# Six value-row buffers in place of eight, and six kept selection weight units in place of four, in a two-block transformer kernel

## The reference, cut to what matters

```python
def peer(h, w_query, sub_keys, u, v):        # per chunk of 16 tokens
    q = einsum('btd,dq->btq', hx, w_query)   # 1024 -> 2048
    s = einsum('bthpc,hpnc->bthpn', q, sub_keys)
    ...                                      # top-16 per half, then top-16 of 256
    u_sel = take(u, expert, axis=0)          # 128 rows of 1024 per token
    v_sel = take(v, expert, axis=0)
    act = gelu(einsum('btd,bthkd->bthk', hx, u_sel))
    return einsum('bthk,bthkd->btd', gate * act, v_sel)
```

## Time and profile before

| | |
|---|---|
| Median of 3 runs | 2071.33 us (2069.29 to 2072.9) |
| Profiled execution | 2071.07 us |
| Span of that execution, first to last instruction | 2069.3 us |
| TensorE / VectorE / ScalarE / GpSimd busy | 86% / 66% / 41% / 50% |
| Moved by DMA | 704.86 MB, of which the gathers 553.72 MB |
| Gathers | 528 of u and 528 of v |
| Ring loads | 246 |

### The profile page before, as it was taken

How to read it: one execution, slowest core, us unless ns; L and a number is a source line. 1 busy time by engine, 2 the same in 40 slices (tenths; PEclk the granted TensorE clock), 3 DMA queues, 4 the chain that set the end, 5 groups by cost and what they waited for, 6 DMA issues and landing times.

```text
span 2069.3 us, 21820 instructions
## 1 busy us (share of the span) xinstructions
PE 1787.2 (86%) x6516; PEld 1010.4 (49%) x6516; DVE 1356.4 (66%) x2953; ACT 846.8 (41%) x2015; POOL 1044.7 (50%) x1064
## 2 busy tenths in 40 slices
PE   9899777779988787797989878977778999989998
PEld 6565222213344452244546424422223986778996
DVE  4577988556488569847956975355554566558874
ACT  3344434330157134314732434344333445546653
POOL 0666777775567657755766676667773000000000
PEclk9999999999999999998999999999999999999999
DMA  7999999999999999999999999999996744445564
GB/s 279 366 407 408 409 409 409 406 398 368 378 403 381 409 409 409 409 410 386 384 399 409 409 409 409 409 406 409 410 409 261 232 157 122 135 147 150 189 185 132
DMA packets 194709, 704.86 MB, mean 341 GB/s; under 512 B 21769, under 2 KB 23313, under 8 KB 194337
## 3 DMA queue, kind: packets, MB, share of 16 engines
q0 software_dynamic: 152064, 553.72, 67.9%
q1 hardware_dynamic: 40816, 147.51, 20.6%
q10 hardware_dynamic: 1712, 2.24, 0.3%
HBM read 701.66 MB, written 1.06 MB: 340 GB/s over the span
## 4 chain that ended last, share of the span: by engine, by line
PE 43%; DMA 29%; POOL 10%; DVE 8%; issue 6%; ACT 2%; ACTq 0%; DVEq 0%; SPq 0%; POOLq 0%
PE ps L950 18%; DMA a<-in_peer_v,eidx 16%; DMA a<-in_peer_u,eidx 13%; PE ps L668 12%; POOL a L498 5%; PE ps L574 5%; POOL a L510 5%; DVE a L1916 3%; PE ps L691 3%; PE ps L813 2%; DVE ring_r L2100 1%; PE ps L703 1%; PE ps L627 0%; DVE a L2054 0%; PE ps L560 0%
## 5 line engine op out<-in xcount | busy, mean ns | idle before, releaser
L668 PE MATMUL ps<-a,diag 128*128 128x512 f32 (+1 forms) x1880 | 911.5, 617 | 217.0 <-DMA a<-in_peer_v,eidx 178.8
L1916 DVE SCALAR_TENSOR_TENSOR a<-a,ps 128x1024 f32<-128x1024 f32 x512 | 621.4, 1218 | 378.8 <-DMA a<-in_peer_u,eidx 359.1
L668 PEld LDWEIGHTS ps<-a,diag 128*128 128x128 f32 (+1 forms) x1880 | 331.3, 190 | 743.3 <-issue 651.6
L498 POOL DMA_INDIRECT a<-in_peer_u,eidx x528 | 525.5, 995 | 311.2 <-DVE a L1916 143.1
L510 POOL DMA_INDIRECT a<-in_peer_v,eidx x528 | 518.4, 982 | 221.4 <-issue 123.3
L1269 ACT ACTIVATE gel<-dots 128x1 f32<-128x1 f32 x528 | 104.3, 201 | 691.8 <-DVE a L1916 686.8
L950 PE MATMUL ps<-a_r 128*128 128x256 f32 (+1 forms) x1624 | 381.1, 328 | 6.2 <-DVE a_r L2324 2.4
L950 PEld LDWEIGHTS ps<-a_r 128*128 128x128 f32 x1624 | 270.2, 189 | 37.7 <-DVE a_r L2324 2.8
L2100 DVE TENSOR_TENSOR ring_r<-wring,a_r 128x1024 fp32r<-128x1024 f32 x139 | 169.6, 1222 | 127.4 <-ACT a_r L1523 127.1
L1523 ACT ACTIVATE a_r<-wring 128x1024 fp32r<-128x1024 f32 x139 | 146.3, 1053 | 71.0 <-PE ps L950 62.2
L1281 ACT ACTIVATE diag<-cstc,cga 128x128 f32<-128x128 f32 (+1 forms) x398 | 158.3, 398 | 13.3
(11 more groups left out here) (292 smaller groups left out, 1550.0 us busy)
## 6 DMA issues: line engine op xcount, KB each, us to landing
wring<-in_units SPq DMA_DIRECT2D x246, 512.0 KB, 4.4
a<-in_peer_u,eidx POOLq DMA_INDIRECT x528, 12.9
a<-in_peer_v,eidx POOLq DMA_INDIRECT x528, 13.0
late<-in_units SPq DMA_DIRECT2D x8, 512.0 KB, 15.5
a<-in_units SPq DMA_DIRECT2D x7, 512.0 KB, 14.6
a<-in_poolm SPq DMA_DIRECT2D x1, 1632.0 KB, 8.5
late<-in_cs SPq DMA_DIRECT2D x1, 1280.0 KB, 7.6
h<-in_xin SPq DMA_DIRECT2D x2, 512.0 KB, 4.3
```

Of the source, the lines that this page charges most:

```text
L498: g.indirect_dma_start(ug[:, n % NU, :], None, peer_u, bass.IndirectOffsetOnAxis(ap=eidx[:, t, k:k + 1], axis=0))\
L668: last = nc.tensor.matmul(ps[0:P, b + j, :], diag[:, pe_slots[n] % ND, 0:P], vg[:, k % NV, j * 512:(j + 1) * 512], start=False, stop=n == ...
L1916: v.scalar_tensor_tensor(ug[:, n % NU, :], ug[:, n % NU, :], 1.0, hnm if t == 2 else ps2(4), ALU.mult, ALU.mult, accum_out=dots[:, k % 8:k ...
```

## The change

Two of the eight v buffers are given up. Their 2048 words a partition, which lie behind the six others in `a1`, become `kept_too`, places for two more kept units; `a1` keeps its size. Units 10 to 15 of the query projection are now loaded once for both fronts. The two new ones (10 and 11) are loaded by SyncE in the start of the kernel, behind the last of the units with places of their own, with no wait ahead of them; units 12 to 15 go to `late` as before, at their place in SyncE's order. The v buffer of slot n is now n modulo 6, and a v gather waits for the slot six before it. The semaphore `kept` counts six loads. The ring carries four units less: two in front A, two in front B.

```diff
-NV = 8
+NV = 6
+NK = 6
...
-        A1W = (NU + NV) * 1024
+        A1W = (NU + NV + NK - 4) * 1024
...
-        vg = a1[:, NU * 1024:A1W].rearrange("p (n d) -> p n d", d=1024)
+        vg = a1[:, NU * 1024:(NU + NV) * 1024].rearrange("p (n d) -> p n d", d=1024)
...
+        kept_too = a1[:, (NU + NV) * 1024:A1W].rearrange("p (n d) -> p n d", d=1024)
...
-        KEPT = {U0["wq" + x] + 12 + m: m for x in "AB" for m in range(4)}
+        KEPT = {U0["wq" + x] + 16 - NK + m: m for x in "AB" for m in range(NK)}
...
             if n in KEPT:
-                return kept[:, KEPT[n]:KEPT[n] + m, :]
+                k = KEPT[n]
+                return kept_too[:, k:k + m, :] if k < NK - 4 else kept[:, k - NK + 4:k - NK + 4 + m, :]
...
+                if n == U0["wq"] + 14:
+                    for m in range(NK - 4):
+                        k = U0["wqA"] + 16 - NK + m
+                        sp.dma_start(kept_too[:, m, :], units[in_dram[k], :, :]).then_inc(S("kept"), 16)
...
                 if n in KEPT:
-                    if n < U0["wqB"]:
+                    if n < U0["wqB"] and KEPT[n] >= NK - 4:
                         sp.wait_ge(S("sc0_pe"), PEER_H + 1)
                         sp.dma_start(weights(n)[:, 0, :], units[in_dram[n], :, :]).then_inc(S("kept"), 16)
...
-            def sums_slot(P, k, n, vfill, b=6):
+            def sums_slot(P, n, b=6):
...
-                pe.wait_ge(S(f"v{k % NV}"), vfill)
+                pe.wait_ge(S(f"v{n % NV}"), 16 * (n // NV + 1))
...
-                                            vg[:, k % NV, j * 512:(j + 1) * 512], start=False,
+                                            vg[:, n % NV, j * 512:(j + 1) * 512], start=False,
```

More of the change, by code:

```diff
@@ L684, in beside @@
             def beside(base):
-                return Beside(lambda k: sums_slot(128, k, base + k, 16 * ((base + k) // NV + 1)), LAG)
+                return Beside(lambda k: sums_slot(128, base + k), LAG)
             def q_unit(w, j, a, b):
@@ L764, in _ @@
             for k in range(16):
-                sums_slot(META, k, m_base + k, 16 * ((m_base + k) // NV + 1), META_BANK)
+                sums_slot(META, m_base + k, META_BANK)
             sums_end(2, 2, META_BANK)
```

## The result

The changed kernel takes 2084.55 us (median of 4 runs, 2083.63 to 2089.76), the kernel before 2070.54 us in the same series: a ratio of 1.0074, interval 1.0062 to 1.0085, or 14 us slower. Forecast were 2076.3 us and a range of 2066 to 2081 us: the sign was right, the size was not. The profiled execution took 2083.63 us, with a span of 2081.8 us against 2069.3.

What follows compares the result with a forecast made beforehand. Full DMA engines were taken as the bound, in some not-full stretches TensorE or GpSimd's issues. Front A -2.6 + 1.1 = -1.5, front B +3.3 + 3.4 = +6.7, together +5.2 on 2071.1: 2076.3 us, range 2066 to 2081.

Steps and rivals of the forecast that it cites:

- The wait where TensorE is the bound, cost 0: 480 to 570 us: later v gathers cost 0, covered by full TensorE and VectorE's 12.5 us wait; uncovered +5.1 us.
- Rival 3: 480 to 570 us: VectorE's lost lead is not swallowed, coefficients reach TensorE late, 5.1 us on top: 2081 us; chance 0.12.
- Slot 306, +3.3: Front B, gather issued at 968.4 us: refill lands at 979.0 instead of 975.7, +3.3 us, bounds 0 and 4.3.
- three places are left: Only at slots 194, 306 and 363 does the refill land later than before: +1.1, +3.3 and +3.4 us.
- Slot 363, +3.4: Front B's query units: issue waits until 1142.5 us, lands at 1148.7 instead of 1145.3, +3.4 us that stays.
- Front B's -2.6: Two ring loads fewer in front B save 2.6 us of DMA time, counted as nothing because the queue runs empty.
- Front A's -2.6: Two ring loads fewer in front A's burst, where DMA is full, come out whole: -2.6 us.
- Slot 194, +1.1: Gather issued at 611.4 us moves to 614.7, lands at 620.9 instead of 619.8: +1.1 us that stays.
- The prologue's loads, cost 0: Two added loads, issued at some 24 us, find room before the first gather at 50 us: cost 0; uncovered +2.6 us.
- Full stretches, cost 0: Where DMA is full, six v buffers just cover its pace and later gathers stand shorter in the queue: cost 0.
- the 405 that the prediction named as a sign of being wrong: A rate below 405 GB/s in the full stretches would show six buffers too few for the pace.
- The fit of the Trainium skill: 2.0 us and bytes / 436e3, 3.2 us per gather; the three costs would be 0, 0.3 and 0.4 us; not used.

Runs made afterwards that it cites:

- depth alone: Six v buffers instead of the eight of the kernel before, four kept units as there, nothing loaded in the prologue: 2087.59 us, ratio 1.0074.
- experiment 4: Kernel before, with only the v gathers of slots 194, 306 and 363 to 365 also waiting for the slot six before: 2077.14 us, ratio 1.0039.
- v6_clean: Six v buffers and four kept units against the kernel before, in a series where that took 2070.92 us: 2087.59 us (2 runs), ratio 1.0074.
- front A alone: Kernel before, with only the v gathers of slots 150 to 190 also waiting for the slot six before: 2075.17 us, ratio 1.0022.
- seven and seven: Seven u and seven v buffers in place of six and eight, four kept units, against the kernel before: 2074.3 us, ratio 1.0022.
- v6: Six v buffers, four kept units, the rest as in the changed kernel; against the kernel before, ratio 1.0043 in the first series, later 1.0074.
- experiments 2 and 1: Both ran six v buffers with four kept units against the kernel before: 2 gave 1.0074; 1, where DMA was short, 1.0037 to 1.0064.
- experiments 4 and 6: 4: three places' v waits tightened in the kernel before, 1.0039. 6: V_BEHIND 3 and 1 in the changed kernel, 1.0053 and 1.0144; 3 in the kernel before, 1.0057.
- v6_again: Repeat of six v buffers and four kept units against the kernel before, in a series where that took 2179.79 us: ratio 1.0037.

## Why the prediction was wrong in size

Point by point, by its steps:

- **The wait where TensorE is the bound, cost 0: this step failed.** It measured +6.4 us (6.6 in depth alone, 4 to 5 with the stretch tightened alone, 2 to 7 by that experiment's interval). The text had the right quantity, two slots less ahead, 4 gathers, 5.1 us, and then let VectorE's 12.5 us wait swallow it. That wait gave VectorE its time back, not the DMA engines. They are full behind it, 410 GB/s in 570 to 603 us, so 5.4 us of gathers that were not moved are still missing when VectorE's 30 us of work on rows in hand are used up. Rival 3 had the place and nearly the price; its condition (VectorE's lag not swallowed, so coefficients late at TensorE) was half right: the lag was swallowed, but the rows were late, the v rows at TensorE (2.52 us) and the u rows at VectorE (4.47 us), and behind these a coefficient too (2.33 us for 1.07). TensorE waited for none of it inside the stretch.
- **Slot 306, +3.3: the place was right, the term too small.** Alone it gives 4.0 up to slot 328, by the lateness of GpSimd's stream and not of its own row. But the whole stretch gives +8 in the changed kernel, where slot 327 waits again, between the slots 320 and 332 that have no slack. The prediction took "three places are left" from times of before, in which a slot with slack counts as safe; slack is spent by the delay before it.
- **Slot 363, +3.4: right in size,** +3.5 measured, +3.6 alone, with the luck told in experiment 4.
- **Front B's -2.6 counted as lost: right.** The changed kernel's lead over v6_clean does not grow in front B, it falls from 4.1 to 2.4 us.
- **Front A's -2.6: 4.1 us at slot 290** by the same comparison, of which 2.4 us survive front B; both are differences of two executions, good to some 2 or 3 us.
- **Slot 194, +1.1: wrong, 0 in the ladder.** In experiment 4 its refill was issued at 614.1 us and landed after 5.6 us, not 6.2, at 619.7 us; before it was 619.8.
- **The prologue's loads, cost 0: right.** Issued at 24.9 us, landed at 39.7 and 41.3, in the gap where the rate rose from 64 to 140 GB/s; the first gather comes at 49.6 us, and slot 150 ends 0.2 us later than before.
- **Full stretches, cost 0: right in 76 to 460 us** (407 GB/s, v rows landing after 10.9 us in 250 to 350 us, 11 forecast), not quite in 676 to 960: 405 GB/s, with the dip at 860 to 930 us whose cause is open. Its 16 x 70 us = 1.12 MB are 2.7 us by the division above, but the ladder moves by 0.8 us only from slot 240 to 290. 1060 to 1580 us has 404, below the 405 that the prediction named as a sign of being wrong; the 79 x 35 us = 2.8 MB missing in 1130 to 1165 us, slot 363's dip, account for it.
- **The fit of the Trainium skill** ("DMA: Bandwidth & Descriptors", "Anatomy of one DMA") would have made the three places cheaper still, 0.7 us. Slot 363's refill in experiment 4 landed after 4.1 us, the quickest of all v gathers of that trace, still above its 3.2; the measured terms of 4.0 and 3.6 us decide against it.

The missing 9 us, by the changed kernel's ladder: 6.4 for the first step; less 1.1 for slot 194; nothing for front A (from +6.4 at slot 186 to +3.8 at 305, the forecast 2.6); 4.9 for front B's stretch (from 3.8 to 12.0, 8.2 for 3.3); 0.1 for slot 363; less 1.2 that come back behind slot 372, for which no run gives a reason. That is 9.1; 5.2 + 9.1 = 14.3 us, the ladder's last row. It is a sum over one execution and closes by its making; the experiments bear out its two large terms, the first step and front B's stretch.

## What to carry to other kernels

In this kernel, whose gather phase ends with full DMA queues, the price of a buffer was near the DMA time that the engines stood idle more, and neither an engine that was busy all through the stretch nor a wait that another engine had in it hid it. Read the GB/s column of a full-TensorE stretch as a debt that the next saturated stretch may not repay. As an estimate it is good to 1 to 3 us here: 5.1 us for v6_clean's first stretch (6.6 in the ladder), 6.5 for front A alone (3.8 to 4.9), 4.5 for seven and seven (3.1), and 2.7 against 0.8 in 860 to 930 us. When places of small slack are listed, walk them in order with the delay already accumulated, and look for the consumers that use a row the moment it lands.

## What was not expected of the hardware

- The DMA engines moved 405 GB/s in 76 to 460 us in one trace of the kernel of `v6` and 366 in another (experiments 2 and 1). The mean granted clock of TensorE over these executions was 0.973 and 0.946. It is not the chip: on one and the same the kernel before took 2070.1 and 2164.16 us (experiments 4 and 6). What lowers the rate stays open; no run was made to settle it.
- A v gather of 512 KB landed in 4.1 us (slot 363 in experiment 4), where the quickest of the kernel before took 5.1.
- The profiled execution can be the quickest of its series by some 3 us (2073.4 against a median of 2077.14).
- A wait "with no releaser" can be one of the profile's making. In v6_again's trace ScalarE waits 273 us before its gelu for "issue", a line that the trace at 405 GB/s does not have:

```profile
ACT gel L1276 <- DVE a L1923: 456.3, 215, 15.4
ACT gel L1276 <- issue: 273.1, 164, 5.8
```

Together the two lines are 729.4 us in 379 waits. In v6_clean, the same kernel, ScalarE waits there for VectorE alone, 714.4 us in 401 waits. So it looks like the same wait, put down in part to no one, and not like a cause of the longer time.
